# A fused decoder step on one core: in the MLP, the weight block W22 is brought once per group of products and the first weight sum moves to the start of the group

## The reference

```python
    x = x + jnp.concatenate([ya, yb], axis=-1) @ w_out
    x = x + _cross_attn(_rms(x, norm_attn), mem_k, mem_v, w_q, w_o)
    hm = _rms(x, norm_mlp) @ w_up                       # 2048 -> 8192
    x = x + jnp.square(jax.nn.relu(hm)) @ w_down        # 8192 -> 2048
```

## Time and profile before

| | |
|---|---|
| time, median of 3 runs (lowest, highest) | 2670.58 us (2669.82, 2670.86) |
| the profiled execution: time | 2676.77 us |
| the profiled execution: span of the core | 2675.1 us |
| TensorE busy | 2624.5 us, 98% of the span |
| VectorE busy | 1769.5 us, 66% |
| ScalarE busy | 1008.5 us, 38% |
| weight loads into the raw buffers | 482, 512 KB each |
| loads of W22 into SUMW (one more into SUM0) | 63, 512 KB each |

### The profile page before, as it was taken

One profiled execution on the slowest core, in us unless ns is written; L12 is line 12 of the kernel. 1 busy time (PEld: TensorE's weight loads), 2 busy tenths in 40 slices (PEclk: granted clock), 3 DMA queues, 4 the chain that ended last, 5 costly groups with the idle time before them and its releaser, 6 DMA issues.

```text
span 2675.1 us, 48780 instructions
## 1 busy us (share of the span) xinstructions
PE 2624.5 (98%) x20404; PEld 2559.6 (96%) x20404; DVE 1769.5 (66%) x2166; ACT 1008.5 (38%) x1297; POOL 152.9 (6%) x235
## 2 busy tenths in 40 slices
PE   8999999999999999999999999999988999999997
PEld 8989999999999997979999999999988999999996
DVE  7646533344443233257988888888877888888887
ACT  6532211211331121123655565565533333333344
POOL 1100000000000001000001000000010000000000
PEclk9999999999999999999999999999999999999998
DMA  8763222222224445433377766666696666566653
GB/s 283 227 219 99 93 87 87 86 86 86 88 79 155 145 147 219 170 139 132 138 246 247 253 240 235 221 238 227 221 331 230 239 223 212 202 213 234 223 164 107
DMA packets 139594, 486.32 MB, mean 182 GB/s; under 512 B 12672, under 2 KB 18944, under 8 KB 131232
## 3 DMA queue, kind: packets, MB, share of 16 engines
q1 hardware_dynamic: 105616, 293.08, 33.1%
q0 software_dynamic: 33808, 190.79, 19.2%
HBM read 402.96 MB, written 80.86 MB: 181 GB/s over the span
## 4 chain that ended last, share of the span: by engine, by line
PE 93%; DVE 3%; DMA 3%; issue 1%; ACT 1%; SPq 0%; DVEq 0%; POOL 0%; ACTq 0%
PE psum_main L1649 39%; PE psum_main L2007 27%; PE psum_side L2007 20%; PE psum_main L1756 3%; DMA unit_raw<-weights 2%; PE psum_main L1933 1%; PE psum_main L1864 1%; DVE unit_low L1331 1%; PE psum_side L1829 1%; PE psum_side L1905 1%; DMA cache_low_a<-cache_v 0%; ACT unit_high L799 0%; DMA mem_raw<-mem_t 0%; DVE residual L1620 0%; PE psum_side L1916 0%
## 5 line engine op out<-in xcount | busy, mean ns | idle before, releaser
L799 ACT ACTIVATE unit_high<-unit_raw 128x1024 fp32r<-128x1024 f32 x384 | 402.3, 1055 | 546.1 <-DVE unit_raw L1352 119.2
L1649 PE MATMUL psum_main<-inner_a,unit_high 128*128 128x272 f32 x3584 | 599.9, 289 | 0.0
L1331 DVE TENSOR_TENSOR unit_low<-unit_raw,unit_high 128x1024 fp32r<-128x1024 f32 x384 | 469.2, 1222 | 110.1 <-ACT unit_high L799 110.1
L634 ACT ACTIVATE unit_high<-unit_raw 128x1024 fp32r<-128x1024 f32 x226 | 239.3, 1060 | 738.8 <-PE psum_main L1649 683.4
L1649 PEld LDWEIGHTS psum_main<-inner_a,unit_high 128*128 128x128 f32 x3584 | 507.2, 188 | 3.5 <-issue 3.4
L958 DVE TENSOR_TENSOR unit_low<-unit_raw,unit_high 128x1024 fp32r<-128x1024 f32 x226 | 276.4, 1225 | 239.2 <-ACT unit_high L634 237.4
L2007 PE MATMUL psum_main<-hidden,unit_high 128*128 128x272 f32 x2048 | 392.3, 290 | 11.4 <-DVE residual L1498 11.3
L2007 PE MATMUL psum_main<-tokens,unit_high 128*128 128x272 f32 x2048 | 388.5, 288 | 1.7 <-DVE hidden L1468 1.0
L1649 PE MATMUL psum_main<-inner_a,unit_low 128*128 128x272 f32 x1792 | 369.9, 287 | 0.0
L2007 PEld LDWEIGHTS psum_main<-hidden,unit_high 128*128 128x128 f32 x2048 | 324.7, 190 | 12.8 <-DVE residual L1498 12.5
L2007 PEld LDWEIGHTS psum_main<-tokens,unit_high 128*128 128x128 f32 x2048 | 321.8, 189 | 2.4 <-DVE hidden L1468 1.5
(11 more groups left out here) (221 smaller groups left out, 3350.7 us busy)
## 6 DMA issues: line engine op xcount, KB each, us to landing
unit_raw<-weights SPq DMA_DIRECT2D x482, 512.0 KB, 4.0
hidden_kept<-hidden_staged POOLq DMA_DIRECT2D x32, 1904.0 KB, 7.3
hidden<-hidden_kept POOLq DMA_DIRECT2D x56, 1088.0 KB, 8.0
unit_sum<-weights SPq DMA_DIRECT2D x63, 512.0 KB, 4.2
residual_kept<-residual POOLq DMA_DIRECT2D x32, 272.0 KB, 5.2
cache_ring_t<-cache_k POOLq DMA_DIRECT2D x8, 1024.0 KB, 8.1
cache_low_a<-cache_v POOLq DMA_DIRECT2D x8, 1024.0 KB, 12.3
cache_ring_a<-cache_k POOLq DMA_DIRECT2D x8, 1024.0 KB, 6.8
```

What stands on the lines that cost most here:

```text
L634: act.activation(WHI[:, s, :], RAW[:, s, :], ACT.Copy).then_inc(high_ready, 1)
L799: act.activation(WHI[:, slot, :], raw, ACT.Copy).then_inc(mlp_high, 1)
L1331: dve.tensor_tensor(WLO[:, slot, :], raw, WHI[:, slot, :].bitcast(F32), ALU.subtract) \
L1649: ins = pe.matmul(out, weights_at(w), moving, start=first and n == 0, stop=last and n == len(passes) - 1)
```

## The change

W22 is no longer loaded twice in the groups 1 to 63: `SUMW` is written by `sum_1` from RAW[3] and RAW[2], and SyncE's loads into SUMW (lines 423 and 434) are gone. `sum_1(q)` so waits for the load of RAW[3], which is the last of its group. On VectorE, `sum_1` and `sum_3` of a group move from inside the group before to its own beginning, ahead of `sum_2`. Group 0 stays as it was.

```diff
@@ SyncE
                 else:
-                    if q == 1:
-                        sp.wait_ge(mlp_ready, 5)
-                        sp.dma_start(into(q, RAW[:, 2, :]), w21).then_inc(mlp_raw[2], 16)
-                    else:
-                        sp.wait_ge(mlp_ready, PRODUCTS * (q - 1) + 4)
-                        sp.dma_start(into(q, SUMW[:, :]), w22).then_inc(mlp_raw[4], 16)
-                    if q > 1:
-                        sp.wait_ge(mlp_ready, PRODUCTS * (q - 1) + 5)
-                        sp.dma_start(into(q, RAW[:, 2, :]), w21).then_inc(mlp_raw[2], 16)
+                    sp.wait_ge(mlp_ready, PRODUCTS * (q - 1) + 5)
+                    sp.dma_start(into(q, RAW[:, 2, :]), w21).then_inc(mlp_raw[2], 16)
                     sp.wait_ge(mlp_sum, 4 * q)
                     sp.dma_start(into(q, RAW[:, 0, :]), w11).then_inc(mlp_raw[0], 16)
                     sp.wait_ge(mlp_ready, PRODUCTS * (q - 1) + 6)
                     sp.dma_start(into(q, RAW[:, 1, :]), w12).then_inc(mlp_raw[1], 16)
-                    if q == 1:
-                        sp.wait_ge(scale_ready, 1)
-                        sp.wait_ge(sums_done, 4)
-                        sp.dma_start(into(q, SUMW[:, :]), w22).then_inc(mlp_raw[4], 16)
                     sp.wait_ge(mlp_ready, PRODUCTS * q)
                     sp.dma_start(into(q, RAW[:, 3, :]), w22).then_inc(mlp_raw[3], 16)
@@ VectorE
             def sum_1(q):
                 dve.wait_ge(mlp_raw[2], 16 * (q + 1))
-                dve.wait_ge(mlp_raw[4], 16 * (q + 1))
-                total = SUMW[:, :] if q else SUM0[:, :]
-                dve.tensor_tensor(total, total, RAW[:, 2, :], ALU.add).then_inc(mlp_sum, 1)
+                if q == 0:
+                    dve.wait_ge(mlp_raw[4], 16)
+                    dve.tensor_tensor(SUM0[:, :], SUM0[:, :], RAW[:, 2, :], ALU.add).then_inc(mlp_sum, 1)
+                else:
+                    dve.wait_ge(mlp_raw[3], 16 * (q + 1))
+                    if q == 1:
+                        dve.wait_ge(sums_done, 4)
+                    dve.tensor_tensor(SUMW[:, :], RAW[:, 3, :], RAW[:, 2, :], ALU.add).then_inc(mlp_sum, 1)
@@
-            sum_1(1)
-            sum_3(1)
 
             for q in range(1, 2 * QUADS + 1):
                 if ahead:
+                    sum_1(q)
+                    sum_3(q)
                     sum_2(q)
@@
-                if q + 1 < 2 * QUADS:
-                    sum_1(q + 1)
-
@@
                 if q + 1 < 2 * QUADS:
-                    sum_3(q + 1)
                     low(q + 1, 1)
```

## The result

| | before | after |
|---|---|---|
| time, median of 4 runs (lowest, highest) | 2670.47 us (2669.82, 2670.86) | 2752.25 us (2743.78, 2757.79) |
| profiled execution: time, span | 2676.77, 2675.1 us | 2752.47, 2750.8 us |
| ratio after / before, 95% interval | | 1.0299 (1.0285 to 1.0314) |

A forecast was written before the change was run, and what follows sets the result against it. TensorE's pace was taken to bound the MLP outside the turn. Parts 1 to 4 gave 26.0 + 6 + 0 + 2 = +34 us, 2710.8 us profiled, carried to the median as 2704.6 us; range 2687 to 2724 us.

The forecast's parts named there:

- What bounds the kernel: MLP: TensorE sets the pace without gaps outside the 95 us turn; shortening VectorE's or DMA's work there gains nothing.
- Part 1, the chain: Down groups: two more sums ahead of product 2 make each group 0.93 us longer, 26.0 us over 28 groups.
- the rule from the Trainium skill: Down groups' chain: semaphores between chained VectorE instructions cost nothing extra, so steps take 1.14 us and the chain costs 17.6.
- Part 3, the up groups: Up groups: TensorE could start product 2 0.21 us ahead of need, so 0 us; bounds 0 and 9 us.
- Part 4, the turn: Group 1 and groups 32 to 35: waits move from product 6 to product 2; +2 us, bounds -4 and +8.
- Part 2, W22 later than the chain: Down groups: sum_1 waits for W22, due 7.07 us after issue; 6 us taken, bounds 0 and 12.8 us.
- The relief: Down groups: 0.4 us off each of 18 landings over 7.07 us, one load in five of a 2 us queue.
- Rival (b): Down groups: the removed load does not help W22, which competes with hidden values; +43 us, 2713 us, chance 0.22.

The follow-up runs named there:

- e2: Changed kernel, with the loads of hidden values that GpSimd issued at the end of product 3 issued at the end of product 5; 2708.9 us, ratio 1.0141.
- e4: Changed kernel with other sums: sum_3 in its old place, SUMW = W22 + RAW[2], RAW[0] = SUMW - W11, W11 loaded ahead of W21; 2669.2 us.
- e1: Kernel before, with sum_1 and sum_3 moved as in the change, but W22 still loaded twice; 2711.3 us, ratio 1.0146.
- e9: Changed kernel with the load of W22 into SUMW kept in its old place, waited for by VectorE but unused; 2733.3 us, ratio 1.0226.
- e10: Changed kernel, with the loads of hidden values that wait for product 3 waiting for add_down(q, 3), some 0.8 us later; 2754.6 us, ratio 1.0301.
- e7: Changed kernel, with the loads of hidden values of product 3 issued at low(q, 6), 1.6 us later; 2715.0 us, ratio 1.0169.

## Why the prediction was wrong

**What bounds the kernel** held. TensorE's pace is the MLP's, 9.04 us of three products was the budget, and removed traffic bought nothing.

**Part 1, the chain**: right in mechanism and size. 6.84 and 9.97 us came out to the hundredth, with the 1.32 and 1.26 us steps; the rule from the Trainium skill ("VectorE: DVE Perf Modes", section "The DRAIN you can't avoid"), which gave 17.6 us, does not fit. Measured by e2, the chain costs 31.0 us against 26.0. A period with the wait is 22.12 against 21.09 us, 1.03 and not 0.93, since product 2 behind a wait takes 0.1 us longer (3.28 against 3.18 us); in the periods that were 21.04 us it is 1.07. The last of the 28 periods, with squares of the final norm on VectorE, is 2.3 us longer.

**Part 3, the up groups**: right. 0.21 us of slack was enough: the up groups differ by 0.4 us in all.

**Part 4, the turn**: the kind of change was right, and the size came out better than taken because gain and loss cancelled, -1.0 where +2 was. Before's waits of 3.5 and 5.6 us ahead of product 6 are gone, and product 2 waits 4.8 and 5.6 us instead. With one sum behind W22 (e4) the turn is 5.7 us shorter than before, and product 2 still waits there, up to 4.4 us.

**Part 2, W22 later than the chain, is the step that failed.** The sum had 6 us for it, the bound was 12.8, and the runs show 43.6 (after 664.4 less e2 620.8). Three things were wrong in it:

1. *The relief had the wrong sign.* I took off 0.4 us per slow group because a load in front was gone; neither the 0.4 nor the queue of 2 us behind it was read from a row. W22's median landing rose from 7.4 to 8.0 us. (By the formula of the Trainium skill, "DMA: Bandwidth & Descriptors", section "Anatomy of one DMA — SWDGE (gpsimd) path", which is fitted to transfers issued by GpSimd, this load would take 3.2 us and this part would be nothing. The trace does not agree, with a median of 8.0 us.) Summed over the 28 down groups, what W22 exceeds 7.07 us by is 14.1 us before, 16.0 in e1, 12.8 in e9 and 22.6 in the changed kernel. The new order issues W12 1.85 us ahead of W22 in most groups and no longer 3.0, but e1 and e9 have that too. What adds the 10 us to e9's 12.8 is the missing load, and by what means the runs do not show.
2. *Only one load was considered.* W12 lands after 7.1 us or more in 10 of the 23 groups 37 to 59, up to 9.7 us, and holds `low(q+1, 1)` and with it `sum_1`; in e9 it never takes over 6.7. Of the 19 groups in which `sum_1` is late, W12 sets its start in 9 and W22 in 10. Together they make `sum_1` 30.6 us late, some 8 more than W22 alone would.
3. *The clock was left out.* The sum counted a gap at its length. Behind gaps of 2.0 us and more (in e1, e9 and e10 also of 1.7 to 1.9) product 2 often ran partly at the lower clock level, 4.8 us in place of 3.27: 8 groups, 13.1 us. Gaps of up to 1.4 us in before had shown nothing of the kind, and I took the lower clock of the turn for a matter of its waits of up to 5.6 us alone.

This closes the sum: over the 28 groups product 2 begins 30.8 us later than the chain alone would have it, and 30.8 + 13.1 is 43.9 against 43.6 us measured. The sign that the prediction named for part 2, VectorE's wait for RAW[3] between nothing and 13 us, came to 7.9 us (2060 to 2650 us) and would not have shown the failure: it sees neither W12 nor the clock. Rival (b), "W22 is the bound", had the place right and took 12.8 us, the landings of before, for the worst. The landings of before were measured while nobody waited for them, and a bound taken from them was no bound: in the changed kernel the loads stand elsewhere.

My first explanation after the result, that W12 was the cause (theory L), fell with e1 and, in its finer form O, with e10. What stands: the condition for the extra loss is that `sum_1` waits for the load issued last (e9 against e1: 18.4 us), beside hidden values (e2: all of it gone), with three sums behind the landing and not one (e4: nearly all of it gone, although its loads also stand elsewhere). With all loads in place this is worth 21.6 us over the chain (e9 against e2); the other 22.0 us come only when the load in front is missing.

Left open: why the unused load of e9 brings both W12 (at most 6.7 against 9.7 us) and W22 (7.5 against 8.0 us, median) in earlier, and with it half of the loss beyond the chain. The number of loads alone is not the reason: e4 has the same four, with W11 issued some 3 us sooner, and there W12 lands after 3.8 and W22 after 7.1 us (medians). e10 rules out a mere lead of W12 over the hidden values as the whole answer, because there W12 came in time and W22 still later.

## What to carry to other kernels

A load whose first user moves from far behind to the head of a chain has to be judged by its landing in the busiest stretch and by the slack of the whole chain, not by the bytes that go away; and the landing read before the change is only a first guess, since the change moves the issues too. When a second copy is to be dropped, look for an algebra in which the late operand enters last: here one sum in place of three behind it made 3% of loss into none. Where a gap on TensorE may pass some 2 us, add the slower matmuls that may follow it to the price.

## What was unexpected of the hardware

- Fewer bytes in flight did not bring the others in sooner: with a fifth of the weights' traffic gone, W22's median landing was 8.0 us against 7.5 with the unused load kept (e9). With the same four loads but W11 issued some 3 us sooner it was 7.1 (e4).
- W22's 512 KB landed after 5.0 us when the 1088 KB were issued 0.3 to 0.4 us behind them (e7), after 8.3 us when issued some 0.8 us ahead of them (e10), and after 8.0 us when 1.5 to 1.6 us ahead (the changed kernel); all medians.
- Gaps of TensorE of 1.7 to 4.0 us were often followed by a slow product 2, 4.8 us in most cases; where it was looked at, the granted clock over it was 0.62 on average, that is, mostly at 1.2 in place of 2.4 GHz. Behind others of 1.9 to 3.2 us product 2 kept its time: it took 3.27 us behind a gap of 2.84 us at 2572 us and 4.80 us behind one of 2.84 us at 2335 us. What decides it the runs do not show.
